# The feed-forward features of each layer in chunks of 6, 8 and 8 tiles, where they were 8, 8 and 6

## The reference, cut to what matters

```python
for l in range(2):
    x = x + 0.5 * swiglu(rmsnorm(x, ffn1_norm[l]), ffn1_w_gate[l], ffn1_w_up[l], ffn1_w_down[l])
    x = x + mixer(rmsnorm(x, mix_norm[l]))      # layer 0: gated convolution, layer 1: attention
    x = x + 0.5 * swiglu(rmsnorm(x, ffn2_norm[l]), ffn2_w_gate[l], ffn2_w_up[l], ffn2_w_down[l])
y = rmsnorm(x, final_norm)

def swiglu(x, w_gate, w_up, w_down):            # w_gate, w_up: 1024 x 2816, w_down: 2816 x 1024
    return (silu(x @ w_gate) * (x @ w_up)) @ w_down
```

## Time and profile before

| | |
|---|---|
| Time of the runs | 2139.5 us median of 3 (2136.0 to 2141.06) |
| The profiled execution | 2136.56 us; its span 2134.7 us |
| TensorE busy | 2088.5 us (98%), 15154 matmuls |
| VectorE, ScalarE, GpSimd busy | 1281.3 us (60%), 944.7 us (44%), 201.8 us (9%) |
| Chain that ended last | TensorE 86%, VectorE 6%, ScalarE 3%, DMA 3% |
| Mean granted clock of TensorE | 0.996 of full speed |

### The profile page before, as it was taken

One profiled execution on the slowest core, in us unless ns is written; L12 is line 12 of the kernel. 1 busy time (PEld: TensorE's weight loads), 2 busy tenths in 40 slices (PEclk: granted clock), 3 DMA queues, 4 the chain that ended last, 5 costly groups with the idle time before them and its releaser, 6 DMA issues.

```text
span 2134.7 us, 37128 instructions
## 1 busy us (share of the span) xinstructions
PE 2088.5 (98%) x15154; PEld 2011.5 (94%) x15154; DVE 1281.3 (60%) x1621; ACT 944.7 (44%) x1597; POOL 201.8 (9%) x259
## 2 busy tenths in 40 slices
PE   8999999999999999999999999999999899999997
PEld 7999999999989999999899999988888889999997
DVE  6745636578566556365764655565655467466465
ACT  5524425456445345154552533543444445244252
POOL 1101000011001010000100100100011001010000
PEclk9999999999999999999999999999999999999999
DMA  7745545457347455444554644422213247365451
GB/s 223 172 116 145 153 100 153 132 145 173 104 133 178 139 130 158 100 123 144 152 165 107 150 144 119 148 91 82 84 57 120 58 133 180 101 159 148 104 144 45
DMA packets 135416, 278.08 MB, mean 130 GB/s; under 512 B 15632, under 2 KB 20032, under 8 KB 135248
## 3 DMA queue, kind: packets, MB, share of 16 engines
q1 hardware_dynamic: 90304, 192.45, 27.7%
q0 software_dynamic: 30976, 57.53, 16.9%
q10 hardware_dynamic: 13968, 25.72, 3.5%
HBM read 268.55 MB, written 7.09 MB: 129 GB/s over the span
## 4 chain that ended last, share of the span: by engine, by line
PE 86%; DVE 6%; ACT 3%; DMA 3%; issue 2%; ACTq 0%; DVEq 0%; POOL 0%; POOLq 0%
PE ps L1383 39%; PE ps L1500 30%; PE ps L1393 7%; PE ps L1636 5%; DMA stage<-w 3%; ACT w_hi L663 2%; DVE w_lo L992 2%; PE ps L1614 1%; DVE neg_max L1283 1%; DVE scores L1280 1%; PE ps L1565 1%; ACT probs L913 1%; PE ps L1596 1%; DVE stage L1001 1%; PE ps L1400 0%
## 5 line engine op out<-in xcount | busy, mean ns | idle before, releaser
L663 ACT ACTIVATE w_hi<-stage 128x1024 fp32r<-128x1024 f32 (+1 forms) x446 | 464.7, 1042 | 614.8 <-PE ps L1500 387.0
L992 DVE TENSOR_TENSOR w_lo<-stage,w_hi 128x1024 fp32r<-128x1024 f32 (+1 forms) x446 | 537.5, 1205 | 284.7 <-ACT w_hi L663 280.8
L1383 PE MATMUL ps<-xa_hi,w_hi 128*128 128x288 f32 x1280 | 379.4, 296 | 2.4 <-ACT u L701 2.4
L1500 PE MATMUL ps<-hid_hi,w_hi 128*128 128x288 f32 x1664 | 380.5, 297 | 0.8 <-DVE hid_lo L1299 0.8
L1500 PE MATMUL ps<-hid_lo,w_hi 128*128 128x288 f32 x1664 | 378.1, 296 | 0.0
L1500 PE MATMUL ps<-hid_hi,w_lo 128*128 128x288 f32 x1664 | 377.9, 296 | 0.0
L1383 PE MATMUL ps<-xa_lo,w_hi 128*128 128x288 f32 x1280 | 377.9, 295 | 0.0
L1383 PE MATMUL ps<-xa_hi,w_lo 128*128 128x288 f32 x1280 | 376.8, 294 | 0.0
L1383 PE MATMUL ps<-xb_hi,w_hi 128*128 128x288 f32 x1200 | 358.4, 299 | 10.8 <-DVE up L1056 6.9
L1383 PE MATMUL ps<-xb_lo,w_hi 128*128 128x288 f32 x1200 | 354.3, 295 | 0.0
L1383 PE MATMUL ps<-xb_hi,w_lo 128*128 128x288 f32 x1200 | 353.2, 294 | 0.0
(11 more groups left out here) (123 smaller groups left out, 2439.7 us busy)
## 6 DMA issues: line engine op xcount, KB each, us to landing
stage<-w SPq DMA_DIRECT2D x460, 256.0 KB, 3.8
stage<-w SPq DMA_DIRECT2D x104, 512.0 KB, 3.9
stage<-w POOLq DMA_DIRECT2D x200, 256.0 KB, 4.9
w_raw<-w ACTq DMA_DIRECT2D x80, 256.0 KB, 3.1
stage<-w SPq DMA_DIRECT2D x32, 384.0 KB, 3.8
x<-x_t SPq DMA_DIRECT2D x8, 288.0 KB, 5.0
k_t<-k_sb ACTq DMA_DIRECT2D x8, 288.0 KB, 2.1
v_t<-v_sb ACTq DMA_DIRECT2D x8, 288.0 KB, 2.5
```

The lines of the kernel that those rows point to most:

```text
L663: act.activation(prepared(w_hi, b), raw_of(b), ACT.Copy).then_inc(w_hi_done, 1)
L992: dve.tensor_tensor(prepared(w_lo, b), raw_of(b), prepared(w_hi, b).bitcast(F32), ALU.subtract).then_inc(w_ready, 1)
L1383: mm = pe.matmul(ps[:, bank, 0:HALF], wt[:, b % W_SLOTS, w], xt[:, k, :], start=(start and k == 0 and n == 0), stop=(k == KQ - 1 and n == ...
L1500: mm = pe.matmul(ps[:, bank + i, 0:HALF], wt[:, b % W_SLOTS, w], xt[:, k, cols(h)], start=(k == 0 and n == 0), stop=(k == p.k - 1 and n == 2))
```

## The change

The chunks are 6, 8 and 8 tiles, so the phase `first` of every feed-forward layer has six tiles, and `next` and `last` have eight. (The opening of the convolution's phase keeps its eight.) With six tiles `early_order` is P1 0, P1 1, P1 2, P2 0, P1 3, P2 1, P1 4, P2 2, P1 5, P2 3, P2 4, P2 5: twelve products in six batches. The first split batch, which then belongs behind the sixth product, is written behind the operand copies that follow the seventh, and the two seeds stand behind P2 4 and P2 5.

```diff
-FFN_CHUNKS = (8, 8, 6)
+FFN_CHUNKS = (6, 8, 8)
...
                     else:
                         act.activation(est[:, j, 0:HALF], ps[:, EARLY_BANKS[j % 4], 0:HALF],
                                        gate).then_inc(c11_done, 1)
-                    split_hi(p.run[kind, j])
+                    if e != 5 or p.n == DT:
+                        split_hi(p.run[kind, j])
                     if e == 0:
...
                     if e == 6:
                         operand_hi(n, 5, diff_done, diffs + 3)
                         operand_hi(n, 6, diff_done, diffs + 4)
-                    if kind == "P2" and j in (p.n - 3, p.n - 2):
-                        s = j - (p.n - 3)
+                        if p.n < DT:
+                            split_hi(p.run[early_order(p.n)[5]])
+                    seed_at = 5 if p.n == DT else 4
+                    if kind == "P2" and j in (seed_at, seed_at + 1):
+                        s = j - seed_at
                         act.wait_ge(c11_done, p.c11s + s + 5)
                         seed(p, s, est[:, s, HALF:TOK])
```

## The result

The changed kernel takes 2152.2 us (median of 6 runs, 2148.7 to 2156.4), the kernel before 2139.9 (6 runs): a ratio of 1.0065, 95% interval 1.0048 to 1.0083, or 10 to 18 us slower. The forecast was 2156. The profiled execution took 2152.24 us, 15.7 more than that of before, with the same 15.7 between the spans.

The account below looks back on a forecast made before the run. TensorE, busy 2088.5 of 2134.7 us, was taken to bound the kernel. -5.2 + 21.1 + 5.6 - 4.3 = +17.2 us on 2136.56, plus 2.9 for the runs' median, gave 2156.7, written 2156; range 2145 to 2166.

Parts of the forecast that it names:

- Part 1: Four feed-forward openings: 16 plain products become 12, moved tiles' products split; TensorE's work falls 5.2 us, added splits cost nothing.
- Part 2: Each feed-forward opening: TensorE's twelfth plain product waits for ScalarE's eviction, 4.78 to 6.71 us a layer, 21.1 us in all.
- the chain named: In the opening: VectorE's norm work, then its sums, ScalarE's two weight splits, the eviction queued behind them, TensorE's twelfth product.
- Part 3: After the four new waits: TensorE's clock falls, costing 1.4 us each, 5.6 us in all, bounds 0 and 7.2.
- Part 4: Closing phase, 8 hidden tiles for 6: waits for sums of squares shrink, 4.3 us saved, including 0.3 from last sum's clock.
- the late part starves: Rival, late part: split products start sooner but reloaded weights don't, losing 4.2 us; 2161, up to 2165 us; chance 0.13.
- the lengths of the openings: Sign: opening stretch 1.4 to 2.8 us shorter in three layers, about as long as before in the first.

Follow-up runs that it names:

- e3: Changed kernel with VectorE making the first two split groups' sums before inverting the norm (first layer: behind the differences); 2138.5 us, ratio 0.9995.
- e1: Changed kernel with the eviction of tile 5's first product put ahead of both weight splits; 2149.3 us, ratio 1.0041.
- e2: Changed kernel with all opening evictions and both seeds ahead of second, third and fourth weight split, first behind the tenth product's eviction; 2148.7 us, ratio 1.0039.
- e5: Changed kernel with dummy matmuls of ones (20, in the first layer 29) on TensorE before the twelfth product; 2151.6 us, ratio 1.0048.
- e7: e3 with late part's first sum and split behind tile 0's evictions; first layer's sums unmoved, its ScalarE opening order as in e2; 2139.8 us, ratio 0.9994.
- e10: e3 with a third place in store for P4's second weight piece, loaded ahead of P5's; 2135.8 us, ratio 0.9978.
- e13: e10 with the pieces loaded in the old order (P5's ahead of P4's); 2137.2 us, ratio 0.9999.
- e9: e2 with a third place in store for P4's second weight piece, loaded ahead of P5's; ratio 1.0039.
- e11: Kernel before with chunks of 8, 6 and 8 tiles and a third place for P4's second weight piece, loaded ahead of P5's; 2126.2 us, ratio 0.9935.
- e4: Kernel before with chunks of 8, 6 and 8 tiles and nothing else changed; 2130.8 us, ratio 0.9953.
- e12: e11 with the pieces loaded in the old order (P5's ahead of P4's); 2126.1 us, ratio 0.9942.

## Why the prediction was right, point by point

**Part 1** (-5.2): the counts are as foreseen, 512 plain matmul records for 640, 454 weight splits for 446. TensorE has no wait of over 0.5 us in the gate and up products of the feed-forward layers' later chunks, so the added splits cost nothing that shows.

**Part 2** (+21.1): 6.61, 4.67, 4.67 and 4.67 us, 20.6 in all, from the chain named. e3 shows its head (make the sums sooner and the wait is gone), e1 and e2 its tail (ScalarE's order).

**Part 3** (+5.6) is the term that was mis-sized, and beyond its upper bound of 7.2. The twelfth product took 3.59, 3.59, 3.34 and 3.59 us until the first split product, 6.4 us more than four times 1.940. The slow stretch did not end there: the first thirty split matmuls took 0.71, 1.26, 0.35 and 0.87 us longer than at their usual pace, each 0.17 of which the kernel before has too; 2.5 us more. Together 8.9. Against the same stretches of e5, where the clock stayed up, it is 9.0. I had taken the price of one row (1.79 us over two products, of which a part already ran fast) for the most that a wait can cost. The Trainium skill's TensorE: Matmul & The Clock Gate (HAM oscillation), by which all four pay, agrees with the four stretches at 0.50 to 0.56.

**Part 4** (-4.3): 0.81 and 1.60 us of the two waits in the third layer, 1.76 in the last: -4.2. The last sum kept its clock and took 0.75 us for 1.30, another -0.5 where I had 0.3.

**What was not in the sum.** -5.2 + 20.6 + 8.9 - 4.7 = 19.6, and the spans differ by 15.7. Smaller waits make up 4.5 us of the difference: `up` 3.6 us for 6.9, L701 2.1 for 2.4, and the attention's wait for `probs_t` 4.5 for 5.4. Against that the first three products of the first layer, which are the same in both kernels, took 8.54 us for 7.61 (mean granted clock 0.69 for 0.78), 0.9 us more. So the two errors, the clock's 3.3 us too low and these 4.5 us not seen, nearly cancelled: the time was hit better than the terms, and that was luck.

They may be linked. The rival "the late part starves" was right on the mechanism and wrong on the place. In the changed kernel, with its long wait, VectorE's waits for pieces halve (10.6 us for 20.4): the wait seems to give the loads time. This is the likely reason that the wait's price can't simply be had back: e1, e2 and e5, which shorten the opening by 7.2, 23.0 and 5.8 us, pay 5.3, 19.5 and 10.2 us in the late part, and VectorE's waits for pieces rise to 20.2, 22.0 and 25.7. In e2 a trace names the reloads; for e1 and e5 no run adds the place to them. Only with the sums made sooner (e3, e7, e10, e13) is the loss gone (0.9978 to 0.9999 for 1.0065). The third place shortens the late parts by 6.5 to 11.6 us in all five kernels that have it, but lengthens the rest by 4.4 to 7.8, and against its counterpart no one of them is clearly faster: e9 is level with e2 and e13 with e3, and the intervals of e10 and e3, of e11 and e4 and of e12 and e4 overlap.

Of the signs listed, the lengths of the openings were off: that of the first layer was to be about as long as before and is 1.8 us longer, about half of it from the slow first products, and the rest because the wait and the clock behind it are longer than the four products taken out; the three others are 1.1, 1.5 and 1.1 us shorter, two of them below the range of 1.4 to 2.8.

## What to carry to other kernels

Where a first stage is made shorter, look at which of its instructions stand in front of a chain that does not get shorter, and read from the old trace the time at which that chain ends: here it gave the wait within 3%. Before a wait is taken away, ask what its time lets arrive; taking ScalarE's queue out of a wait of 20.6 us (e2) gave back little (1.0039 for 1.0065, on intervals that overlap): in its trace the places freed by the stage's own splits have to be refilled first. Making the late input sooner (e3) gave the whole loss back. When a wait is gone from one engine's list, look for it in the others': a third place took VectorE's waits for pieces and gave ScalarE new ones. And a change of two effects is best split: six tiles in the middle and eight at the end (e4, 0.9953) were worth having, six in the opening were not, not even with sums and place improved (e10 at 0.9978, e11 at 0.9935).

## What the runs showed of the hardware

The slow clock behind a wait cost 1.6 to 2.7 us each time (sum 8.9), on top of the idle time, and it differed between equal waits: three of 4.67 us cost 2.7, 1.6 and 2.4. Split matmuls were 0.240 us apart in it, 0.134 outside. With dummy matmuls in the wait (e5) the granted clock stayed at 1.00 and the cost was gone. e2's waits for L705 are shorter: behind those of 2.98, 3.07 and 3.83 us the clock fell too, behind that of 2.87 it stayed at 1.00, as it did behind the 2.64 us before the changed kernel's last sum.
